# Hybrid GDN and sliding-window layer: attention queries stored without padding, logits as two 64 by 64 quarter products per chunk

## The reference, cut to what matters

```
qc = q.reshape(B, NC, CHUNK, Hkv, G, D)
kb = band_keys(k.reshape(B, NC, CHUNK, Hkv, D), NC)
logits = jnp.einsum('bnqhgd,bnshd->bnhgqs', qc, kb).astype(jnp.float32) * (D ** -0.5)
logits = logits + bias.astype(jnp.float32).reshape(Hkv, G, CHUNK, S)
```

## Time and profile before

| | |
|---|---|
| median of 3 runs | 3086.01 us (3085.89 to 3086.07) |
| profiled execution | 3087.55 us, its span 3085.7 us |
| TensorE busy, matmul | 2983.1 us (97%), 17064 records |
| TensorE busy, weight load | 2558.4 us (83%) |
| VectorE busy | 1424.5 us (46%) |
| ScalarE busy | 1052.9 us (34%) |
| GpSimd busy | 416.3 us (13%) |
| granted TensorE clock, mean | 0.997 of full speed |

### The profile page before, as it was taken

The page is one execution under the profiler, slowest core; times in us unless marked ns, Lnnn a source line. Parts: engine busy times, 40 slices in busy tenths (PEclk is TensorE's granted clock), DMA queues, the critical chain, the costliest instruction groups (busy, mean ns, idle before and its releaser), DMA issues.

```text
span 3085.7 us, 43710 instructions
## 1 busy us (share of the span) xinstructions
PE 2983.1 (97%) x17064; PEld 2558.4 (83%) x17064; DVE 1424.5 (46%) x3013; ACT 1052.9 (34%) x2993; POOL 416.3 (13%) x237
## 2 busy tenths in 40 slices
PE   6999999999999999999999999999999999999997
PEld 5888888888888888888888888888888888888886
DVE  4676666523255555532235555552223555554112
ACT  3444444432234433331114433343112343343100
POOL 3332233343201000100000000100000001100000
PEclk9999999999999999999999999999999999999998
DMA  6444343488633222345552222324555223222463
GB/s 221 163 168 146 125 142 133 160 300 307 239 136 111 84 98 98 111 150 205 192 220 98 89 104 101 113 96 164 213 186 191 98 98 111 101 96 96 167 222 142
DMA packets 77532, 462.79 MB, mean 150 GB/s; under 512 B 13072, under 2 KB 17296, under 8 KB 29200
## 3 DMA queue, kind: packets, MB, share of 16 engines
q1 hardware_dynamic: 65520, 429.42, 38.9%
q10 hardware_dynamic: 11808, 30.57, 2.7%
HBM read 356.15 MB, written 103.81 MB: 149 GB/s over the span
## 4 chain that ended last, share of the span: by engine, by line
PE 83%; issue 8%; DVE 4%; ACT 3%; DMA 0%; POOL 0%; DVEq 0%; POOLq 0%; SPq 0%
PE bank L1074 18%; PE bank L1076 18%; PE bank L1075 18%; PE bank L1179 6%; PE bank L1193 5%; PE bank L1183 5%; PE bank L1217 2%; PE bank L1168 2%; PE bank L1203 2%; PE bank L1263 1%; ACT area L618 1%; PE bank L1157 1%; PE bank L1255 1%; PE bank L1210 1%; DVE area L841 1%
## 5 line engine op out<-in xcount | busy, mean ns | idle before, releaser
L1074 PE MATMUL bank<-hT_hi,w_sl 128*128 128x512 f32 x2144 | 896.1, 418 | 1.1 <-DVE hT_lo L765 1.0
L1076 PE MATMUL bank<-hT_hi,w_sl 128*128 128x512 f32 x2144 | 840.3, 392 | 0.0
L1075 PE MATMUL bank<-hT_lo,w_sl 128*128 128x512 f32 x2144 | 837.2, 391 | 0.0
L1076 PEld LDWEIGHTS bank<-hT_hi,w_sl 128*128 128x128 f32 x2144 | 402.4, 188 | 87.8
L1074 PEld LDWEIGHTS bank<-hT_hi,w_sl 128*128 128x128 f32 x2144 | 405.0, 189 | 60.5 <-ACT hT_hi L459 1.4
L1075 PEld LDWEIGHTS bank<-hT_lo,w_sl 128*128 128x128 f32 x2144 | 405.5, 189 | 58.8
L902 DVE TENSOR_TENSOR area<-bank,area 128x512 f32<-128x512 f32 x192 | 132.8, 692 | 398.4 <-PE bank L1193 397.5
L360 POOL TENSOR_TENSOR w_sl<-w_raw,w_sl 128x1024 fp32r<-128x1024 f32 x91 | 219.9, 2416 | 527.9 <-ACT w_sl L433 527.9
L841 DVE SCALAR_TENSOR_TENSOR area<-zraw,stc,area 128x512 f32<-128x512 f32 x288 | 232.7, 808 | 4.3
L1179 PEld LDWEIGHTS bank<-area 128*128 128x128 f32 x1536 | 198.2, 191 | 29.7 <-issue 15.6
L373 POOL TENSOR_TENSOR rqo<-qo,half 128x8 f32<-128x8 f32 x32 | 64.6, 2018 | 1085.9 <-DVE qo L983 1085.9
(11 more groups left out here) (183 smaller groups left out, 4580.3 us busy)
## 6 DMA issues: line engine op xcount, KB each, us to landing
w_sl<-saved_w SPq DMA_DIRECT2D x273, 1024.0 KB, 4.8
saved_w<-w_sl SPq DMA_DIRECT2D x91, 1024.0 KB, 4.8
w_raw<-in_w_tiles SPq DMA_DIRECT2D x91, 512.0 KB, 5.7
area<-in_x ACTq DMA_DIRECT2D x8, 2048.0 KB, 10.3
out_y<-area ACTq DMA_DIRECT2D x4, 2048.0 KB, 7.2
bias_sb<-in_bias ACTq DMA_DIRECT2D x33, 128.0 KB, 2.7
fw<-in_final_w ACTq DMA_DIRECT2D x1, 512.0 KB, 10.4
stc<-in_step_const ACTq DMA_DIRECT2D x32, 6.5 KB, 2.2
```

Of the source, the lines that this page charges most:

```text
L1074: pe.matmul(dst, a_hi, b_hi, start=first, stop=False)
L1075: pe.matmul(dst, a_hi, b_lo, start=False, stop=False)
L1076: return pe.matmul(dst, a_lo, b_hi, start=False, stop=last)
```

## The change

The queries are kept as they come out of the projection, 128 partitions by 512 positions (`qs_sb`), written by one ScalarE instruction in place of two. Each chunk's logits become two products in place of one: the queries of partitions 0 to 63 with the keys of partitions 0 to 63, into output partitions 0 to 63, and the same for 64 to 127. Each loads 64 rows by 64 columns of the array, at opposite corners, and moves 128 key columns. The buffer's clearing at the start goes, and the count that the engines wait for at the start is 5 in place of 6.

```diff
-        qbd = sb("qbd", [P, 2, NC, P])
+        qs_sb = sb("qs_sb", [P, 2, TB])
...
-            pool.memset(qbd[:, :, :, :], 0.0).then_inc(zeroed, 1)
...
-            pool.wait_ge(zeroed, 6)
+            pool.wait_ge(zeroed, 5)
...
-                zq = bank[bk][:, :].rearrange("p (c t) -> p c t", c=NC)
-                act.activation(qbd[0:DH, par, :, 0:CH], zq[0:DH], ACT.Copy, scale=DH ** -0.5)
-                act.activation(qbd[DH:P, par, :, CH:P], zq[DH:P], ACT.Copy, scale=DH ** -0.5).then_inc(z_read[bk], 1)
+                act.activation(qs_sb[:, par, :], bank[bk][:, :], ACT.Copy, scale=DH ** -0.5).then_inc(z_read[bk], 1)
...
-                        ins = pe.matmul(bch(3)[:, t, :], qbd[:, par, cc, :], kb[:, cc * CH:cc * CH + P], start=True, stop=True)
+                        for lo, hi in ((0, DH), (DH, P)):
+                            ins = pe.matmul(bch(3)[lo:hi, t, :], qs_sb[lo:hi, par, cc * CH:(cc + 1) * CH],
+                                            kb[lo:hi, cc * CH:cc * CH + P], start=True, stop=True)
```

More of the change, by code:

```diff
@@ L462, in _ @@
             act.wait_ge(const_in, 16 * 6)
-            act.wait_ge(zeroed, 6)
+            act.wait_ge(zeroed, 5)
             act.activation(nea[:, :], db[:, 0, :], ACT.Exp).then_inc(const_ready, 1)
@@ L736, in _ @@
         def _(dve):
-            dve.wait_ge(zeroed, 6)
+            dve.wait_ge(zeroed, 5)
             def copy(dst, src):
@@ L1284, in _ @@
             pe.wait_ge(const_in, 16 * 6)
-            pe.wait_ge(zeroed, 6)
+            pe.wait_ge(zeroed, 5)
             pe.wait_ge(x_normed, 1)
```

## The result

The changed kernel took 3101.88 us (median of 5 runs, 3100.48 to 3104.75), the kernel before 3086.07 us beside it: ratio 1.0053, interval 1.0040 to 1.0066. It is 16 us slower, where 42 us were forecast. The direction was right and the time lies in the range, but the rise was forecast at 2.7 times its size.

A forecast was written before the change was run, and what follows sets the result against it. TensorE's own instruction stream was taken to bound the kernel. 7 us for the products plus 35 us for changes of form made 42 us on the profiled 3087.6 us, so 3130 us (median 3128), range 3090 to 3178 us.

The forecast's parts named there:

- The quarters work at once: Logits groups on TensorE: the two quarters' products stream side by side, taken at 0.11 us more per group.
- the price of a change of form: Entering and leaving each logits group: 0.27 us per change, 0.54 us per group, 35 us for 64 groups.
- the 0.163 us: At each change of form: the next record starts only at the last one's end, 0.275 us instead of 0.112.
- the bare load: At each change of form: the next weight load is no longer hidden under a running matmul, 0.11 us more.
- the pairing: Inside a logits group: issue order A A B B leaves first and last records alone, 9 steps, 7 us in all.
- what is absorbed: TensorE's wait for L902: at most 2.7 us absorbed by the longer logits, left out of the sum.
- its own case: Quarters at once with paid changes of form: 3108 to 3142 us, chance 42%.
- the rival with cheap changes: Quarters at once, changes of form free or cheap: 7 us plus up to 15, 3086 to 3108 us, chance 22%.
- Both limits bind at once: Full-array logits records before the change: streaming (about 0.107 us) and weight load (about 0.10 us) both set the 0.112 us step.
- where the next record would have: L1074 behind the logits group before the change: its on-time start was cited for free changes of form.
- One after another: Rival: quarters don't run at once or half loads take full time, 44 to 57 us, up to 92; chance 28%.
- Faster: Rival: both limits lifted, group takes 0.78 us, 7 us less in all, 3079 us, with free changes; chance 5%.

The follow-up runs named there:

- e1: Kernel before with only the new query buffer and its single copy, logits still full-array products: 3084.14 us, ratio 0.9999.
- e2: Kernel before with its padded buffer, two copies and memset kept, only the logits products made quarters: 3102.74 us, ratio 1.0059.
- e3: Changed kernel with each group of quarter products cut in two by a full-array projection step: 3122.88 us, ratio 1.0123.
- e4: Kernel before with each logits group cut in two by the same projection step, as control: 3084.66 us, ratio 0.9998.
- e5: Changed kernel with a group's products reordered, four of the upper quarter first, then four of the lower: 3131.27 us, ratio 1.0151.
- e10: Changed kernel, products ordered by quarters, the lower quarter's moving 64 key columns and the upper's 128: 3107.3 us, ratio 1.0073.
- e8: Kernel before with 64 of 128 key columns moved in its full-array logits products: 3084.88 us, ratio 1.0001.
- e7: Changed kernel with 64 of 128 key columns moved in its quarter products: 3079.44 us, ratio 0.9981.
- e11: Kernel before with each values product split into two of 128 rows by 64 columns moving 64 columns, logits untouched: 3076.52 us, ratio 0.9972.

## Why the prediction was wrong in size

**Right: what bounds the kernel, and what is hidden.** TensorE's stream sets the end; the copy, the memset and the buffer are worth nothing (e1), and all of the rise is in the products (e2).

**Right: the two causes.** The quarters work at once, and the change of form costs; e3 against e4 shows the second by doubling it. The Trainium skill has the rule that a change of tiling mode drains the engine (TensorEngine Tiling (Array Packing), Key Properties). The trace agrees in that each change costs time, 0.09 us and a bare weight load; whether the array is empty in these 0.09 us no record shows.

**Wrong: the price of a change of form.** "One change costs 0.163 + 0.11 = 0.27 us, a group 0.54 us, 64 groups 35 us." The failed step is the 0.163 us: a record's end in the profile was taken as the moment at which the next form can start. It starts 0.20 us after the last record did, not 0.275, so the term is 0.09 us. The other part, 0.11 us for the bare load, was right at the exit: L1072 comes 0.34 us after L1071 in place of 0.23. At the entry it is 0.05 us (a first step of 0.16 in place of 0.11), because that load has 64 columns. So the entry costs 0.14 us and the exit 0.19, which in the table above is 0.17 + 0.02. That is 0.33 us per group in place of 0.54, and 21 us in all in place of 35.

**Wrong: the pairing.** "9 steps of 0.112 us in place of 8, that is 0.11 us more per group, 7 us in all." That took starts to follow the program. They need not (e5, e10). The pairs are complete: eight steps, and these are 0.109 us and not 0.112. With the first step's bare load counted above, the inside of the group costs nothing.

**Left out: what is absorbed.** 2.7 us were named and put aside, and just these came back.

So 35 + 7 - 0 = 42 should have been 21 + 0 - 3 = 18. Measured were 16 us, and 18 us for the same products in e2. All three errors point the same way. The measured 3102 us lies outside the 3108 to 3142 us that the prediction gave its own case and inside the 3086 to 3108 us of the rival with cheap changes. That rival isn't right for it: it allowed the changes up to 15 us, and they cost 21.

**Two rows read wrongly.** "Both limits bind at once" rests on 0.098 us per record with 32 moved columns, an average that has a short first step in it. The first two of those six records, as they stand in the stretch 793.60 to 793.64 us of the trace of before:

```profile
793.53 0.30 PE L1139 MATMUL bank<-sc_all,mk 128*128 128x32 f32 x2
```

The second starts near 793.56, and the other four steps take (794.28 - 0.276 - 793.56) / 4 = 0.11 us. So the full form steps at 0.11 us with 32, 64 and 128 moved columns, and the load is what is left as its limit; the streaming of 128 columns takes the 0.109 us that the quarters show. And L1074 did not start "where the next record would have": that is 893.57 + 8 x 0.112 = 894.47 us, and it started at 894.38. The time comes back in the step behind it (0.32 us in place of 0.23), so a change of type costs nothing, as e4 shows.

**The rivals.** One after another: excluded by the pairs. Free changes of form: excluded by e3. Faster: the full form has a limit that the moved columns don't set (e8), by exclusion its weight load, and the small form lifts that (e7, e11), but with 128 moved columns the streaming binds in nearly the same place, and pairs come 0.109 us apart.

## What to carry to other kernels

A full-array product with zeros in its idle blocks already does the work of two small ones. Against it, dividing the array saved TensorE time here only where the moved operand was narrower than the loaded one: two halves of 64 columns gain with 64 moved columns (5 to 8 us less) and lose with 128 (16 to 18 us more). Each visit to the small form costs 0.33 us between full-array products, so collect small products into long groups. To price it, count visits, take the gap from start to start, and don't take a matmul record's end for the moment at which the next can begin.

## What the runs showed of the hardware

- Records of the two halves start within 0.01 us of each other, and those of one can start ahead of earlier ones of the other, from four records back; alternating them in the program gives eight full pairs (0.82 us), one half after the other 1.31 us.
- Two column halves with all 128 rows in common run at once as well as opposite quarters do (3103.3 and 3102.7 us).
- A change of form delays the next record by 0.09 us and lays one weight load bare: 0.05 us for 64 columns, 0.11 us for 128.
- An fp32 full-array product steps at 0.11 us per record with 128 moved columns, with 64 and with 32: below 128 nothing is gained without a narrower load.
